# Three passes over the rows of a lane in place of three products row by row, in a hybrid decoder trunk in float32 split products

## The reference

```
for i in range(DEPTH):                                   # 2 layers
    x = x + 0.5 * swiglu_ffn(rmsnorm(x, ffn1_norm[i]), ffn1_w_in[i], ffn1_w_out[i])
    h = rmsnorm(x, mix_norm[i])
    mk, mv = jnp.split(mem_n @ mem_w_kv[i], 2, axis=-1)
    z = h @ (hgrn_w_in[j] or gmlp_w_in[j])               # layer 0: HGRN2, layer 1: chunked gMLP
    x = x + concat([o_mix, memory_attention(zx, mk, mv)]) @ w_out
    x = x + 0.5 * swiglu_ffn(rmsnorm(x, ffn2_norm[i]), ffn2_w_in[i], ffn2_w_out[i])
return rmsnorm(x, final_norm)
```

## Time and profile before

| what | value |
|---|---|
| time, median of 3 runs (lowest, highest) | 2415.38 us (2414.51, 2419.41) |
| the profiled execution's own time | 2416.62 us |
| its span, first to last instruction | 2414.9 us |
| TensorE matmuls | 10922, and as many weight loads |
| busy: TensorE, its weight loads, VectorE, ScalarE, GpSimd | 2389.0, 1944.8, 1200.4, 736.7, 287.6 us |
| mean granted TensorE clock | 0.997 |
| read from memory and written | 226.55 and 6.29 MB, 96 GB/s |

### The profile page before, as it was taken

One profiled execution on the slowest core, in us unless ns is written; L12 is line 12 of the kernel. 1 busy time (PEld: TensorE's weight loads), 2 busy tenths in 40 slices (PEclk: granted clock), 3 DMA queues, 4 the chain that ended last, 5 costly groups with the idle time before them and its releaser, 6 DMA issues.

```text
span 2414.9 us, 29569 instructions
## 1 busy us (share of the span) xinstructions
PE 2389.0 (99%) x10922; PEld 1944.8 (81%) x10922; DVE 1200.4 (50%) x1416; ACT 736.7 (31%) x982; POOL 287.6 (12%) x252
## 2 busy tenths in 40 slices
PE   8999999999999999999999999999999999999998
PEld 8978888877888888888878888877788888888876
DVE  6654443346888554444444444334337545444422
ACT  4432222234444322222223222223333222222222
POOL 3400001101333310000110000220001111000021
PEclk9999999999999999999999999999999999999999
DMA  7733333332222333333333333332232233333332
GB/s 223 222 88 96 96 92 91 95 105 62 74 75 70 105 88 96 96 96 95 90 94 95 90 94 96 96 92 91 79 96 79 87 95 89 96 96 96 94 89 79
DMA packets 416931, 233.80 MB, mean 97 GB/s; under 512 B 7668, under 2 KB 409184, under 8 KB 416864
## 3 DMA queue, kind: packets, MB, share of 16 engines
q1 hardware_dynamic: 413680, 223.37, 31.5%
q0 software_dynamic: 3168, 9.50, 1.1%
q10 hardware_dynamic: 16, 0.00, 0.0%
HBM read 226.55 MB, written 6.29 MB: 96 GB/s over the span
## 4 chain that ended last, share of the span: by engine, by line
PE 95%; DVE 2%; ACT 1%; issue 1%; DMA 1%; POOL 0%; ACTq 0%; DVEq 0%; POOLq 0%; SPq 0%
PE acc L853 28%; PE acc L855 28%; PE acc L854 28%; PE acc L612 1%; PE acc L614 1%; PE acc L613 1%; PE mix L244 1%; PE mix L231 1%; PE mix L679 1%; ACT w_hi L1324 1%; DVE tmp L1101 1%; PE mix L379 0%; PE acc L897 0%; PE acc L899 0%; PE acc L898 0%
## 5 line engine op out<-in xcount | busy, mean ns | idle before, releaser
L1035 DVE TENSOR_TENSOR w_lo<-raw,w_hi 128x1024 fp32r<-128x1024 f32 (+1 forms) x424 | 546.8, 1292 | 666.1 <-ACT w_hi L1324 652.4
L853 PE MATMUL acc<-h_hi,w_hi 128*128 128x512 f32 x1920 | 767.9, 400 | 4.0 <-DVE h_lo L1105 3.9
L855 PE MATMUL acc<-h_hi,w_lo 128*128 128x512 f32 x1920 | 757.7, 395 | 0.0
L854 PE MATMUL acc<-h_lo,w_hi 128*128 128x512 f32 x1920 | 757.6, 395 | 0.0
L1324 ACT ACTIVATE w_hi<-raw 128x1024 fp32r<-128x1024 f32 (+1 forms) x424 | 436.7, 1033 | 397.6 <-DMA raw<-in_ffn_w_out_dram 264.0
L853 PE MATMUL acc<-act_hi,w_hi 128*128 128x512 f32 (+1 forms) x1152 | 444.4, 386 | 5.3 <-DVE act_lo L1045 4.2
L855 PE MATMUL acc<-act_hi,w_lo 128*128 128x512 f32 (+1 forms) x1152 | 441.2, 383 | 0.0
L854 PE MATMUL acc<-act_lo,w_hi 128*128 128x512 f32 (+1 forms) x1152 | 441.2, 383 | 0.0
L853 PEld LDWEIGHTS acc<-h_hi,w_hi 128*128 128x128 f32 x1920 | 361.5, 188 | 91.3 <-DVE h_lo L1105 5.2
L854 PEld LDWEIGHTS acc<-h_lo,w_hi 128*128 128x128 f32 x1920 | 361.6, 188 | 85.9 <-issue 3.1
L855 PEld LDWEIGHTS acc<-h_hi,w_lo 128*128 128x128 f32 x1920 | 361.4, 188 | 85.1
(11 more groups left out here) (198 smaller groups left out, 1490.0 us busy)
## 6 DMA issues: line engine op xcount, KB each, us to landing
raw<-in_ffn_w_in_dram SPq DMA_DIRECT2D x176, 512.0 KB, 3.8
raw<-in_ffn_w_out_dram SPq DMA_DIRECT2D x64, 512.0 KB, 4.1
raw<-in_hgrn_w_in_dram SPq DMA_DIRECT2D x40, 512.0 KB, 3.8
raw<-in_gmlp_w_in_dram SPq DMA_DIRECT2D x40, 512.0 KB, 3.7
raw<-in_mem_w_kv_dram SPq DMA_DIRECT2D x32, 512.0 KB, 4.2
raw<-in_ffn_w_out_dram SPq DMA_DIRECT2D x32, 384.0 KB, 3.5
raw<-in_gmlp_w_out_dram SPq DMA_DIRECT2D x24, 512.0 KB, 4.2
raw<-in_hgrn_w_out_dram SPq DMA_DIRECT2D x16, 512.0 KB, 4.1
```

Of the source, the lines that this page charges most:

```text
L853: pe.matmul(bank, w_hi[:, j, i, :], hi, start=(start and i == 0), stop=False)
L854: pe.matmul(bank, w_hi[:, j, i, :], lo, start=False, stop=False)
L855: m = pe.matmul(bank, w_lo[:, j, i, :], hi, start=False, stop=(stop and i == last))
L1035: dve.tensor_tensor(w_lo[:, j, 0:nkb], raw[:, j, 0:nkb], f32(w_hi[:, j, 0:nkb]), ALU.subtract).then_inc(w_lo_ready, 1)
```

## The change

`unit` no longer makes the three products of a row one after the other. It first waits for `w_hi_ready` in place of `w_lo_ready` and runs `w_hi*hi` over all rows, with the waits per row (`each`) in this pass; then `w_hi*lo` over all rows; then it waits for `w_lo_ready` and runs `w_lo*hi` over all rows. The number of products and of weight loads is the same, and so are the three products of each row; the order in which they are added to the bank is another. `v_quad` (line 882) and `v_tensor` (line 597), which write their own loops, stay as they are.

```
             def unit(q, j, operands, bank, start, stop, each=None):
 
-                pe.wait_ge(w_lo_ready, LANES * q + j + 1)
                 last = len(operands) - 1
+                pe.wait_ge(w_hi_ready, LANES * q + j + 1)
                 for i, (hi, lo) in enumerate(operands):
                     if each:
                         each(i)
                     pe.matmul(bank, w_hi[:, j, i, :], hi, start=(start and i == 0), stop=False)
+                for i, (hi, lo) in enumerate(operands):
                     pe.matmul(bank, w_hi[:, j, i, :], lo, start=False, stop=False)
+                pe.wait_ge(w_lo_ready, LANES * q + j + 1)
+                for i, (hi, lo) in enumerate(operands):
                     m = pe.matmul(bank, w_lo[:, j, i, :], hi, start=False, stop=(stop and i == last))
                 m.then_inc(unit_done, 1)
```

## The result

| | before | after |
|---|---|---|
| time, median | 2417.9 us (5 runs) | 2441.8 us (5 runs, 2440.1 to 2443.3) |
| profiled execution, its span | 2416.62, 2414.9 us | 2442.51, 2440.8 us |
| TensorE busy, matmuls | 2389.0 us, 10922 | 2399.4 us, 10922 |
| mean granted clock | 0.997 | 0.994 |

The change made the kernel slower: ratio 1.010, 95% interval 1.0089 to 1.0112, +23.9 us on the medians. The median of before moved up by 2.5 us with more runs; the forecast of 2435.2 stood on 2415.38.

What follows compares the result with a forecast made beforehand. TensorE, busy 2389.0 of 2414.9 us, was taken to bound the kernel. Stalls less the w_lo gain, 15.4 us, plus clock falls, 4.4, gave 19.8 us: 2435.2 us on the median of 2415.38, range 2429.5 to 2442.5.

Steps and rivals of the forecast that it cites:

- Parts 1 and 2: All 8832 products: new neighbours cost 0; in each unit, the added wait for w_lo ahead of the third pass costs 0.
- Rival 3: All 8832 products: passes run tighter, up to 177 us faster (2239 us); chance 0.04.
- Part 3: Units at 74.24 and 129.78 us: the later wait for w_lo gains 0.7 us, nothing elsewhere.
- Part 4: First units with waits per row: row 7 wanted earlier; stalls 3.27, 3.27, 2.93, 3.27, 2.76 and 0.6 us.
- Part 5: Longer idle times at the seams lower TensorE's clock: two falls at 2.2 us each, 4.4 us; ends none or four.
- the two idle times well over 3.78: The two 5.0 us idle times between ffn stages, where falls were forecast; 3.78 us was an early idle with a fall.
- Rivals 1 and 2: 1: stalls but no clock fall, 2430.8 us, chance 0.17; 2: falls at all four places, 2439.6 to 2441.2 us, chance 0.15.
- Rival 4: At the stalled units: delays are given back or don't come, time within 5 us of before; chance 0.06.

Runs made afterwards that it cites:

- run 1: The changed kernel, but units that wait row by row go row by row again as before; all others keep three passes: 2417.5 us, ratio 0.9996 to before.
- run 2: Three passes only in the units that wait row by row, all others row by row as in the kernel before: 2442.6 us, ratio 1.0101 to before.
- run 4: The changed kernel with 19, 19 and 15 added products ahead of row 7's wait in the three longest stalls: 2436.2 us, ratio 1.0076 to before.
- run 5: The changed kernel with 8, 8 and 7 added products ahead of row 7's wait at the same three seams: 2437.7 us, ratio 1.0084 to before.
- run 6: The changed kernel, but in first units of ffn_in, hgrn_in, gmlp_in pass 1 waits only for h_hi, pass 2 for h_lo: 2436.2 us, ratio 1.0080 to before.

## Why the prediction was right or wrong, point by point

- **The sign and the place.** Right: 24 us slower with 20 forecast, all of it in the units with waits per row (runs 1 and 2). 2441.8 us lies only 0.7 us under the upper end of the range, though: nearly all that I had wrong was wrong to the same side.
- **Parts 1 and 2, no cost for new neighbours and one more wait.** Right, by run 1, whose ratio of 0.9996 has all other units in passes, and by the step of 0.2324 us in both traces from 900 to 1200 us. Rival 3 (tighter passes) is out by the same two: to decide anything it wanted 2.2 ns a product.
- **Part 3, 0.7 us for the later wait.** The waits for w_lo are gone in the trace of after and of run 1. From line 917 to the unit that had waited at 129.78 the trace of after is 0.31 us shorter, as forecast; the sum of 0.7 us is below what the times can tell.
- **Part 4, the stalls.** Right to 0.03 us at the three places where the clock stayed up, and to 0.06 us at the three others, by run 4. What was mis-sized is the first unit of all: I took 0.6 us with 1.1 as the far end; the unit ended 1.5 us later (line 843 starts at 19.65 in place of 18.19), 0.2 us of it a later start of the unit. The other 1.2 are just beyond the far end that I gave: the products kept the low clock's step of 0.21 us to the end of the unit and beyond it. The waits for `h_lo` came to 15.2 us where I had about 17, with idle times of 4.55, 4.57, 3.85 and 3.40 us where I had 5.0, 5.0, 4.0 and 3.6: into hgrn_in, 0.3 us of the difference is that row 6 was late as well, so its product held up the first pass (2.12 us for seven products in place of 1.79), and everywhere the idle time is counted from the modelled end, 0.16 us later than I took it. The end of the unit doesn't depend on that. A further wait at 108 us (0.6 us for ScalarE's copy of a bank, line 1355) was not foreseen.
- **Part 5, the clock.** The mechanism was right and is shown by run 4. The count was off: I took two falls, the profiled execution had three, as in run 2. The step that failed is "the two idle times well over 3.78": I used the one idle time of the earlier trace rows as a limit, the third fall came with an idle time of 3.85 us, and run 5 showed falls after 2.7 us. Each fall cost 2.3 to 2.8 us where I took 2.2; the whole term is 7.7 us against 4.4. On the profiled executions 25.9 us stand against the forecast of 19.8: 3.3 of the 6.1 us between them are the clock, 1.7 the start (2.3 against 0.6), and the rest the small terms and the step of the products. On the medians the difference is only 4.1 us, since that of before had moved up by 2.5. (The longest stall of before was 1.66 us, near 1256, and not the 1.58 that the prediction names; nothing hangs on it.)
- **Rivals 1 and 2**, no fall and falls at all four places: neither happened in the changed kernel; run 6 had four. **Rival 4** (given back later): out. No stall after the seams shrank but those that the sum has (w_lo, and 0.2 us of line 917).

The rule of the Trainium skill (TensorE: Matmul & The Clock Gate, section "Why this matters for your kernels") that long idle gaps throw the clock back agrees with the trace at three of the four longest stalls (4.55, 4.57 and 3.85 us), and run 4 took these falls away by work alone. At the fourth, 3.40 us in hgrn_out, the clock stayed up in the changed kernel and fell in runs 4, 5 and 6.

## What to carry to other kernels

When a loop over rows is cut into passes, the wait of the last row moves from the end of a unit to a third of it, and the stall grows by the work that the passes put behind it. Put the operand that comes last at the very end, or take work of the next unit ahead of it, and then look for what started behind the old place (here the norm's product), as it is the next to be late. On TensorE a longer stall may cost its own length and then some more at the lower clock (here 3.3 us of stall and 2.3 to 2.8 of clock), so two kernels with the same sum of work may differ by more than the stall.

## What the runs showed of the hardware that was not expected

- **Whether a stall throws the clock isn't set by its length alone.** The idle time in hgrn_out was 3.4 us in five of these kernels. The clock stayed at 1.00 in the changed kernel and in run 2, and fell in runs 4, 5 and 6. In run 6 an idle of 3.95 us was followed by a fall of 6 to 7 us, one of 4.00 us by a fall of some 3. The shortest idle time with a fall was 2.70 us (run 5), and 2.24 us had none. The untraced executions differ as well: in run 2 the one with the highest mean clock, 0.996, took 2439.7 us and the one with the lowest, 0.991, 2444.0. What decides between these is open.
- **The granted clock's row at the very start can mislead.** In the trace of after the stretch from 16 to 20.5 us reads 1.00, while products of 256 columns take the 0.21 us of the low level. That trace has no record of the clock before 20.6 us, and such a stretch is printed as 1.00:

```profile
16.00:20.50 4.50, 4.50 (x23) 4.50 (x22) 2.77 (x6) 3.69 (x7) 0.00 (x0) 1.00 0.33 95
```
```profile
17.94 1.91 PE L858 MATMUL acc<-act_hi,w_lo 128*128 128x256 f32 x8
```

  (1.91 us from the first start to the last end, with the last product's own 0.4 in it.) The step of the products is the surer sign there.
- **The step of the products has two values**, at the same granted clock, and changes between them in the middle of a run. Starts of a unit's first pass in the trace of after:

```profile
142.90 2.03 PE L853 MATMUL acc<-h_hi,w_hi 128*128 128x512 f32 x8
...
248.87 2.02 PE L853 MATMUL acc<-h_hi,w_hi 128*128 128x512 f32 x8
...
2103.98 2.03 PE L853 MATMUL acc<-h_hi,w_hi 128*128 128x512 f32 x8
...
2204.78 2.03 PE L853 MATMUL acc<-h_hi,w_hi 128*128 128x512 f32 x8
```

  19 units of 24 products in 105.97 us are 0.2324 us each, 18 units in 100.80 us are 0.2333. In the trace of before the slower stretch was near 300 us, in that of after past 1700 us; both orders of the products have both values. If it held for the whole kernel the slower one would cost some 8 us (0.9 ns times 8832, an estimate), more than many a change is worth, and a reason to compare units by their own starts rather than the two spans. Why it changes is open.
